# Sample states of a Mamba-2 layer turned in 32x32 blocks by VectorE instead of by TensorE

## The chip, the cores and the metric

The kernel runs on one core of a Trainium2 chip. The metric is the device time of one launch in microseconds (us). A core has four compute engines with in-order instruction queues of their own, TensorE (PE, matmuls; its weight loads are listed as PEld), VectorE (DVE), ScalarE (ACT) and GpSimd (POOL), and SyncE (SP), which here only issues DMAs. They order their work by semaphores.

## What is computed

One step of a decoder trunk for two groups that share weights: a prompt of 256 tokens, and 8 samples with 4 new tokens each (32 rows). All is float32. The layer is an HGRN2 recurrence and a Mamba-2 recurrence side by side, and then a mixture of 32 experts with the best 4 for each token. The part that matters here is the Mamba-2 recurrence of the samples, each of which brings a state `h0` of 32 heads x 64 x 128:

```
def step(h, inp):                      # one chunk; for a sample the 4 new tokens are one chunk
    xc, dtc, bc, cc = inp
    acum = jnp.cumsum(dtc * a, axis=1)
    ...
    y_inter = jnp.einsum('btgn,bgrpn->btgrp', cc, h) * jnp.exp(acum)[..., None]
    alast = acum[:, -1]
    wdec = jnp.exp(alast[:, None] - acum) * dtc
    h_new = jnp.exp(alast)[..., None, None] * h + jnp.einsum('bsgr,bsgn,bsgrp->bgrpn', wdec, bc, xc)
    return h_new, y_intra + y_inter
```

So each sample's state is read out by C (`y_inter`, a sum over the last axis n of the state), and then decayed and updated (`h_new`).

## The kernel before

The work is staged: the input projections of x, B and C with their convolution (to about 127 us of the span), the Mamba-2 preparation (127 to 160), the loop over the 8 sample states (160 to 256), the loop over 16 pairs of heads of the prompt (256 to 340), HGRN2, the output projections, router and then the experts (from about 621), whose weights stream from HBM through a ring of 9 slots of 2 MB (`wGU`, `wD`).

A state lies in SBUF as `hst[b % 4]`, 128 partitions (two heads x 64) by 16 blocks of 128 state columns n. The sum over n needs n on partitions. So for state b of the loop (`for b in range(NB)` on each engine):

- PE transposes 16 blocks of 128x128 into two PSUM banks in turn (L1905), four at a time, with a projection of the z gate (`project`, L1829, 8 matmuls of 288 columns) between the two halves. It then makes the update of the state (L1915, 16 matmuls in row tiles of 32, into banks 2 to 5), a second projection, and the read-out (L1922): one matmul of 512 columns for each group q of 4 heads' blocks, into the 32 partitions of bank 6 that belong to q. Its weights are `cmk[:, b, q, :]`, C with zeros but for sample b's four columns, so that bank 6 sums up all samples over the loop.
- ACT copies each group of four transposed blocks to `hT` (L1070), copies out the projections (`evacuate`, L1010), and now and then does an exponential or logarithm of HGRN2 (L1084 to L1096).
- POOL multiplies the state in place by its decay (L934) once it is transposed (`r_tr`).
- DVE adds the update out of PSUM to the decayed state (L1360), once POOL is done (`r_dc`) and PE is (`r_up`), then `r_ud`. Before it stands `mask` (L1350, B with the other samples' rows zeroed for the state after). After it come pieces of HGRN2's preparation, written at fixed numbers b: L1364 to L1372 at b = 1, L1374 at 2, the scans L1379 and the copies L1382 and L1383 at 4, L1385 to L1387 at 5, L1390 to L1393 at 6.
- SP stores a finished state and loads state b + 3.

`Steps` helpers such as `dstep` make an engine wait for its own instruction before. After the loop DVE weighs bank 6 by `eA` into `xdt` (L1397), and goes on to the first pair of heads (`bound`, `masked`), for whose matmuls (L1946) PE has two more projections to do first.

Of the kernel before, what the change touches and what calls it, by code (L numbers as in the profile page):

```python
# [89 lines left out]
def build(nc, x_prompt, x_sample, state_hgrn, state_ssm, state_conv, hg_lower_bounds, w_in, hg_norm_w, hg_proj,  # L90
# [24 lines left out]
    with ctx:  # L115
# [335 lines left out]
        cmk = at("cmk", 88, [P, NB, SG, 32])  # L451
# [15 lines left out]
        eA = at("eA", 187.625, [P, HPG])  # L467
# [72 lines left out]
        q_cmk = S("masked_C_ready")  # L540
        q_neg = S("scores_masked_then_identity_ready")
        r_bm = S("masked_B_ready")
        r_tr = S("state_transposed")
        r_tc = S("state_copied")
        r_in = S("state_read_out")
        r_up = S("state_update_ready")
# [201 lines left out]
        with nc.Block() as block:  # L748
# [164 lines left out]
            def _(pool):  # L913
                g = nc.gpsimd
                pstep.on(pool)
                pstep(g.memset(cmk[:], 0.0))
                for b in range(NB):
                    last = g.tensor_copy(cmk[:, b, :, NS * b:NS * b + NS], convBC[:, SG:2 * SG, SEQ + NS * b:SEQ + NS * b + NS])
                last.then_inc(q_cmk, 1)
                pool.wait_ge(q_cmk, 1)  # L920
# [10 lines left out]
                for b in range(NB):  # L931

                    pool.wait_ge(r_tr, 4 * b + 4)
# [65 lines left out]
            def _(act):  # L999
# [30 lines left out]
                evacuate(0)  # L1030
                evacuate(1)
# [4 lines left out]
                for q in range(SG):  # L1036
                    a.activation(eA[32 * q:32 * q + 32, :], av[0:32, 2, HPG * q:HPG * q + HPG], ACT.Exp)
# [24 lines left out]
                for b in range(NB):  # L1062
                    for q in range(4):
                        act.wait_ge(r_tr, 4 * b + q + 1)
                        if b > 0 and q == 0:

                            act.wait_ge(r_in, b)
                        if b == 0 and q == 0:
                            act.wait_ge(q_A, 1)
                        a.copy(hT[:, 4 * q:4 * q + 4, :], ps[:, q % 2, :]).then_inc(r_tc, 1)  # L1070
                        if q == 1:
                            evacuate(I_Z + 2 * b)
# [15 lines left out]
                    if b == 6:  # L1088
                        act.wait_ge(h_ek, 1)
                        a.activation(eT[:], eT[:], ACT.Exp).then_inc(h_x, 1)  # L1090
                    if b == 7:
# [211 lines left out]
            def _(dve):  # L1303
# [25 lines left out]
                v.tensor_scalar(nav[:], av[:], -1.0, None, ALU.mult)  # L1329
                for j in range(12):  # L1330
# [20 lines left out]

                dve.wait_ge(q_xa, 3)
                mask(0)
                for b in range(NB):
# [5 lines left out]
                    v.tensor_tensor(h, h, ps[:, 2:6, :], ALU.add).then_inc(r_ud, 1)  # L1360
                    if b == 1:
# [9 lines left out]
                        dstep(last)  # L1371
# [437 lines left out]
            def _(pe):  # L1809
# [86 lines left out]
                for b in range(NB):  # L1896
                    pe.wait_ge(q_h[b % 4], 32 * (b // 4) + 16)
                    for q in range(4):
# [8 lines left out]
                        if q == 1:  # L1907
                            project(I_Z + 2 * b)
# [482 lines left out]
```

## Time and profile before

| | |
|---|---|
| median of 3 runs | 1547.6 us (1546.91 to 1549.56) |
| span of the profiled execution | 1543.3 us |
| PE, DVE, ACT, POOL busy | 96%, 32%, 18%, 7% of the span |
| loop over the sample states | 160.1 to 255.7 us |
| POOL decays 8 states | 29.1 us |
| DVE adds 8 updates | 18.3 us |

The profile is of one execution. Its times are from the start of the span. A row of a timeline gives start and length in us, engine, line, operation, what is written and read, the shape and how many instructions were merged; in brackets stands the idle time ahead, and what ended it. A float32 matmul stands as two instructions. A matmul's length includes the way through the array, so the starts of successive rows tell how long PE was taken up.

### The profile page before, as it was taken

How to read it: one execution, taken by the hardware profiler on the slowest of the kernel's cores; microseconds unless marked ns; L12 is line 12 of the kernel's file. 1: busy time of each engine (PE TensorE's matmuls, PEld its weight loads, DVE VectorE, ACT ScalarE, POOL GpSimd, SP SyncE). 2: the span in 40 equal slices, each digit the busy share in tenths (PEclk: the TensorE clock that was granted, in tenths of full speed). 3: DMA queues.
4: the chain of work that ended last, by engine and by line, in shares of the span. 5: the costliest groups of instructions: out<-in, count | busy, mean ns of one | idle time of the engine just before them, and what ended most of it. 6: DMA issues, size and time to landing. Idle time of an engine off the chain costs nothing.

```text
span 1543.3 us, 21046 instructions
## 1 busy us (share of the span) xinstructions
PE 1482.6 (96%) x8238; PEld 757.0 (49%) x8239; DVE 490.4 (32%) x955; ACT 277.5 (18%) x618; POOL 110.5 (7%) x98
## 2 busy tenths in 40 slices
PE   9999999999999998999999999999999999899896
PEld 7777777655677764333333333333333333333332
DVE  3652455677350128222222122122122122122123
ACT  1222435532120004211010100101001100100102
POOL 1001222010140702000000000000000000000000
PEclk9999999999999999999999999999999999999998
DMA  6345487546339674999999999999999999999995
GB/s 208 110 163 173 149 262 235 197 137 199 120 103 315 242 298 173 427 427 428 427 428 428 429 428 428 428 428 428 428 429 429 428 428 428 430 428 428 429 428 223
DMA packets 105352, 507.67 MB, mean 329 GB/s; under 512 B 7575, under 2 KB 44031, under 8 KB 80575
## 3 DMA queue, kind: packets, MB, share of 16 engines
q1 hardware_dynamic: 100938, 499.37, 80.7%
q10 hardware_dynamic: 4360, 7.55, 1.5%
q8 instruction: 38, 0.62, 0.2%
q14 instruction: 16, 0.13, 0.0%
HBM read 491.18 MB, written 15.72 MB: 328 GB/s over the span
## 4 chain that ended last, share of the span: by engine, by line
PE 63%; DMA 25%; DVE 2%; ACT 1%; issue 1%; DVEq 0%; SPq 0%; ACTq 0%
DMA wGU<-in_w_gu 23%; PE ps L2325 11%; PE ps L2330 10%; PE ps L1829 10%; PE ps L2312 5%; PE ps L1842 4%; PE ps L2133 3%; PE ps L2147 2%; PE ps L2239 2%; PE ps L2160 2%; PE ps L2273 2%; PE ps L2247 1%; DMA ringS<-in_ssd_proj 1%; PE ps L1905 1%; ACT xs L1273 1%; PE ps L2260 1%
## 5 line engine op out<-in xcount | busy, mean ns | idle before, releaser
L2325 PE MATMUL ps<-wGU,xe 128*64 128x512 f32 x1536 | 342.2, 594 | 17.2 <-DMA wGU<-in_w_gu 16.5
L2330 PE MATMUL ps<-wD,aT 128*64 128x512 f32 x1024 | 226.8, 595 | 0.0
L2325 PEld LDWEIGHTS ps<-wGU,xe 128*64 128x64 f32 x1536 | 107.9, 137 | 232.8 <-issue 198.4
L1829 PE MATMUL ps<-xT,ring 128*128 128x288 f32 x704 | 179.6, 410 | 2.6 <-PEq L199 2.1
L1829 PEld LDWEIGHTS ps<-xT,ring 128*128 128x128 f32 x704 | 130.7, 190 | 42.4 <-issue 5.0
L2330 PEld LDWEIGHTS ps<-wD,aT 128*64 128x64 f32 x1024 | 70.7, 137 | 131.8 <-issue 127.9
L2312 PE MATMUL ps<-wGU,xe 128*64 128x512 f32 x512 | 121.3, 594 | 11.9 <-DMA wGU<-in_w_gu 11.9
L1725 DVE TENSOR_SCALAR sg<-sg 128x512 f32<-128x512 f32 x32 | 13.7, 427 | 333.9 <-ACT sg L1268 333.9
L1732 DVE COPY ysb<-ps 64x512 f32<-64x512 f32 x32 | 22.2, 694 | 304.0 <-PE ps L2334 304.0
L1268 ACT ACTIVATE sg<-ps 128x512 f32<-128x512 f32 x32 | 19.1, 597 | 469.6 <-PE ps L2317 469.6
L391 PE MATMUL ps<-xT,ring 128*128 128x288 f32 x320 | 78.1, 407 | 0.0
L2312 PEld LDWEIGHTS ps<-wGU,xe 128*64 128x64 f32 x512 | 36.4, 136 | 81.5 <-issue 78.4
L391 PEld LDWEIGHTS ps<-xT,ring 128*128 128x128 f32 x320 | 60.6, 190 | 17.1 <-issue 0.5
L2133 PE MATMUL ps<-ynT,ringS 128*128 128x288 f32 x256 | 62.5, 406 | 0.1
L2273 PE MATMUL ps<-ysb,gT 128*128 128x512 f32 x128 | 59.5, 606 | 0.0
L1842 PE MATMUL ps<-ring,xT 128*128 128x512 f32 x128 | 58.3, 600 | 0.0
L1280 ACT COPY ysb<-ps 64x512 f32<-64x512 f32 x32 | 18.5, 578 | 212.9 <-PE ps L2334 212.9
L2133 PEld LDWEIGHTS ps<-ynT,ringS 128*128 128x128 f32 x256 | 48.6, 190 | 13.9 <-DMA ringS<-in_ssd_proj 0.5
L2239 PE MATMUL ps<-hp,psel 128*64 128x512 bf16 x396 | 48.6, 378 | 0.2 <-DVE hp L1687 0.2
L1708 DVE TENSOR_TENSOR yacc<-yacc,ps 128x512 f32<-128x512 f32 x60 | 41.3, 688 | 21.9 <-PE ps L2273 21.9
L2273 PEld LDWEIGHTS ps<-ysb,gT 128*128 128x128 f32 x128 | 22.9, 189 | 35.1 <-issue 35.1
L1842 PEld LDWEIGHTS ps<-ring,xT 128*128 128x128 f32 x128 | 23.3, 190 | 25.7 <-issue 25.3
(476 smaller groups left out, 1451.0 us busy)
## 6 DMA issues: line engine op xcount, KB each, us to landing
wGU<-in_w_gu SPq DMA_DIRECT2D x128, 2048.0 KB, 36.7
wD<-in_w_down SPq DMA_DIRECT2D x64, 2048.0 KB, 36.8
ring<-in_w_in SPq DMA_DIRECT2D x21, 2048.0 KB, 8.8
out<-hst SPq DMA_DIRECT2D x8, 1024.0 KB, 5.8
ringS<-in_ssd_proj SPq DMA_DIRECT2D x4, 2048.0 KB, 10.0
wbuf<-prompt_A_rows ACTq DMA_DIRECT2D x16, 384.0 KB, 3.9
out<-Sb SPq DMA_DIRECT2D x2, 2048.0 KB
ring<-in_hg_proj SPq DMA_DIRECT2D x2, 2048.0 KB, 8.7
```

Of the source, the lines that this page charges most:

```text
L391: last = m.matmul(ps[:, 4 + mt, 0:T], ring[n][:, k, mt * P:(mt + 1) * P], xT[:, k, :], start=(k == 0), stop=(k == KD - 1))
L1708: v.tensor_tensor(y, y, p, ALU.add).then_inc(m_sa, 1)
L1829: last = m.matmul(ps[:, b, 0:T], ring[c % 2][:, k, n * P:(n + 1) * P], xT[:, k, :], start=(k == 0), stop=(k == KD - 1))
L1842: last = m.matmul(ps[:, b, :], xT[:, k, t0:t0 + rows], ring[c % 2][:, k, :], start=(k == 0), stop=(k == KD - 1))
L2133: last = m.matmul(ps[:, 7 - c % 2, 0:T], ringS[n % 2][:, k, (c % 2) * P:(c % 2) * P + P], ynT[:, k, :], start=(k == 0), stop=(k == XT_ - 1))
L2147: last = m.matmul(ps[:, 4 + c % 2, 0:T], ring[n][:, k, (c % 4) * P:(c % 4) * P + P], onT[:, k, :], start=(k == 0), stop=(k == HH - 1))
L2160: last = m.matmul(ps[:, b, :], mT[:, k, t0:t0 + rows], ring[n][:, k, :], start=(k == 0), stop=(k == KD - 1))
L2239: last = m.matmul(ps[half[h], B_X, :], psel[:, t, :], hp0[t][i][:, CW * h:CW * h + CW], start=False, stop=(t == 1 and i == 2))
L2273: return m.matmul(ps[:, bank, :], gT[:, t * P:(t + 1) * P], ysb[j % 2][:], start=True, stop=True)
L2312: last = m.matmul(ps[half[h], bank, :], xe[:, 2 + k, 1, :], wgu[n][:, k, col + CW * h:col + CW * h + CW], start=False, stop=False)
L2325: last = m.matmul(ps[half[h], bank, :], xe[:, f, hx, :], wgu[n][:, k, col + CW * h:col + CW * h + CW], start=(i == 0 and k == 0), stop=False)
L2330: last = m.matmul(ps[half[h], B_Y, :], aT[:, k, i - 4, :], wdn[n][:, k, CW * h:CW * h + CW], start=(i == 4 and k == 0), stop=False)
```

## The change

The state is turned on DVE. One instruction (`v.transpose`, in the program STREAM_TRANSPOSE) turns each 32x32 block of `hst` in its place and writes `hT`: partition 32j + s, block i, columns 32c + r then hold state column n = 32c + s of row 32j + r. It stands in `turn_state(b + 1)`, right after the addition to state b; that of state 0 stands ahead of the loop.

The read-out becomes 64 matmuls for a state: for each row band j, group q and n-block c one of 32 rows by 32 columns of weights, at tile position (32j, 32q), moving 4 blocks of 32 columns; the sum runs over c, and band j goes to bank j of PSUM (banks 0 to 3). Its weights `cT4` are C of all samples, laid out for each band by 16 copies on ACT after `evacuate(0)`. Every sample's rows of C are applied to state b; `gather_inter(b)` on DVE picks sample b's rows by multiplying with the selector `bs2[:, b]` and adds them up in `yin`. The update moves to banks 3 to 6, so the read-out now waits also for the addition (`r_ud`), and the next update for the gathering (`r_iy`). POOL's `cmk` and ACT's copies of `hT` are gone. `eA` is laid out anew by 8 activations instead of 4. HGRN2's pieces are spread otherwise: `kT` (L1372) now at b = 2, four scans at 4 and four at 5 with the copies, L1385 to L1387 at 6, L1390 to L1393 at 7 behind the last gathering, and ACT's exponential of `eT` at 7 instead of 6.

```diff
@@ PE, loop over the states
                 for b in range(NB):
...
-                        for c in range(4):
-                            last = m.transpose(ps[:, q % 2, c * P:(c + 1) * P], hst[b % 4][:, 4 * q + c, :], ident[:])
-                        last.then_inc(r_tr, 1)
-                        if q == 1:
-                            project(I_Z + 2 * b)
-
+                    project(I_Z + 2 * b)
                     pe.wait_ge(r_bm, b + 1)
                     if b > 0:
                         pe.wait_ge(r_ud, b)
+                        pe.wait_ge(r_iy, b)
...
                     project(I_Z + 2 * b + 1)
 
-                    pe.wait_ge(r_tc, 4 * b + 4)
-                    for q in range(4):
-                        last = m.matmul(ps[bands[q], 6, :], cmk[:, b, q, :], hT[:, 4 * q:4 * q + 4, :].rearrange("p c n -> p (c n)"),
-                                        start=(b == 0), stop=(b == NB - 1))
+                    pe.wait_ge(r_tr, b + 1)
+                    pe.wait_ge(r_ud, b + 1)
...
+                    for c in range(4):
+                        for q in range(4):
+                            for j in range(4):
+                                last = m.matmul(ps[bands[q], j, 0:P], cT4[bands[j], q, c, :], hT[bands[j], 4 * q:4 * q + 4, 32 * c:32 * c + 32],
+                                                start=(c == 0), stop=(c == 3), tile_position=(32 * j, 32 * q))
                     last.then_inc(r_in, 1)
@@ DVE
+                def turn_state(b):
+
+                    dve.wait_ge(q_h[b % 4], 32 * (b // 4) + 16)
+                    if b > 0:
+                        dve.wait_ge(r_in, b)
+                    v.transpose(hT[:].rearrange("p i n -> p (i n)"), hst[b % 4][:].rearrange("p i n -> p (i n)")).then_inc(r_tr, 1)
+
+                turn_state(0)
...
+                def gather_inter(b):
+
+                    dve.wait_ge(r_in, b + 1)
+                    part = ps[:, 0:4, 0:P]
+                    whole = yin[:].rearrange("p (j x) -> p j x", j=4)
+                    if b == 0:
+                        v.tensor_scalar(whole, part, bs2[:, 0:1], None, ALU.mult).then_inc(r_iy, 1)
+                    else:
+                        dve.wait_ge(r_iy, b)
+                        v.scalar_tensor_tensor(whole, part, bs2[:, b:b + 1], whole, ALU.mult, ALU.add).then_inc(r_iy, 1)
...
                     h = hst[b % 4][:].rearrange("p (q c) n -> p q (c n)", c=4)
-                    v.tensor_tensor(h, h, ps[:, 2:6, :], ALU.add).then_inc(r_ud, 1)
+                    v.tensor_tensor(h, h, ps[:, 3:7, :], ALU.add).then_inc(r_ud, 1)
+                    if b + 1 < NB:
+                        turn_state(b + 1)
+                    gather_inter(b)
...
-                dve.wait_ge(r_in, NB)
+                dve.wait_ge(r_iy, NB)
@@ POOL
-                    pool.wait_ge(r_tr, 4 * b + 4)
+                    pool.wait_ge(r_tr, b + 1)
@@ ACT
                 evacuate(0)
+                for c in range(4):
+                    for j in range(4):
+                        last = a.copy(cT4[bands[j], :, c, :], convBC[bands[c], SG:2 * SG, SEQ:T])
+                last.then_inc(q_c4, 1)
                 evacuate(1)
```

On PE, one state (b = 0) and the start of the next. Before, with `hst` the state, `ident` the identity, `bm` and `xw` the operands of the update, `xT` and `ring` those of a projection:

```order
91 L1905 MATMUL ps<-ident,hst_912 128x128 x8
92 L1829 MATMUL ps<-xT,ring_67 128x288 x8
93 L1905 MATMUL ps<-ident,hst_912 128x128 x8
94 L1915 MATMUL ps<-bm_919,xw_921 128x128 x16
95 L1829 MATMUL ps<-xT,ring_67 128x288 x8
96 L1922 MATMUL ps<-hT,cmk 32x512 x4
97 L1905 MATMUL ps<-ident,hst_913 128x128 x8
```

Now:

```order
91 L1850 MATMUL ps<-xT,ring_67 128x288 x8
92 L1924 MATMUL ps<-bm_920,xw_922 128x128 x16
93 L1850 MATMUL ps<-xT,ring_67 128x288 x8
94 L1937 MATMUL ps<-hT,cT_917 32x128 x64
95 L1850 MATMUL ps<-xT,ring_67 128x288 x8
```

The sixteen transposes of a state are gone, and four wide matmuls of the read-out have become 64 narrow ones.

On DVE, from the addition to state 1 to that to state 2. Before:

```order
75 L1360 TENSOR_TENSOR hst_913<-hst_913,ps 128x2048
76 L1364 RECIPROCAL lb_952<-lb_952 128x8
77 L1365 TENSOR_TENSOR lb_952<-lb_952 128x8
78 L1366 TENSOR_TENSOR lb_952<-lb_952 128x8
79 L1367 TENSOR_SCALAR lb_952<-lb_952 128x8
80 L1370 TENSOR_SCALAR eT<-eT,lb_952 128x288 x8
81 L1372 TENSOR_SCALAR kT<-eT 128x2304
82 L1350 TENSOR_SCALAR bm_920<-b_922,bs_62 128x128
83 L1360 TENSOR_TENSOR hst_914<-hst_914,ps 128x2048
```

Now:

```order
78 L1378 TENSOR_TENSOR hst_913<-hst_913,ps 128x2048
79 L1328 STREAM_TRANSPOSE hT<-hst_914 128x2048
80 L1362 SCALAR_TENSOR_TENSOR yin<-ps,bs_62,yin 128x512
81 L1385 RECIPROCAL lb_953<-lb_953 128x8
82 L1386 TENSOR_TENSOR lb_953<-lb_953 128x8
83 L1387 TENSOR_TENSOR lb_953<-lb_953 128x8
84 L1388 TENSOR_SCALAR lb_953<-lb_953 128x8
85 L1391 TENSOR_SCALAR eT<-eT,lb_953 128x288 x8
86 L1351 TENSOR_SCALAR bm_921<-b_923,bs_62 128x128
87 L1378 TENSOR_TENSOR hst_914<-hst_914,ps 128x2048
```

The turning of state 2 and the gathering of state 1 now stand ahead of HGRN2's pieces, and POOL's decay of state 2 waits for that turning.

## Rows read from the trace of the kernel before

**Rows 1.** The page: busy time of PE, and GB/s in 40 equal slices.

```profile
PE 1482.6 (96%) x8238; PEld 757.0 (49%) x8239; DVE 490.4 (32%) x955; ACT 277.5 (18%) x618; POOL 110.5 (7%) x98
GB/s 208 110 163 173 149 262 235 197 137 199 120 103 315 242 298 173 427 427 428 427 428 428 429 428 428 428 428 428 428 429 429 428 428 428 430 428 428 429 428 223
```

**Rows 2.** Waits of SP's queue, 540 to 700 us: us, times, longest.

```profile
SPq L818 <- PE ps L2160: 36.5, 2, 26.2
```

**Rows 3.** Timeline of PE, 171 to 184 us: start, length (columns as told above).

```profile
171.03 1.07 PE L1922 MATMUL ps<-hT,cmk 128*32 128x512 f32 x8
172.03 1.09 PE L1905 MATMUL ps<-ident,hst 128*128 128x128 f32 x8
172.95 4.05 PE L1829 MATMUL ps<-xT,ring 128*128 128x288 f32 x16
176.84 1.04 PE L1905 MATMUL ps<-ident,hst 128*128 128x128 f32 x8
177.80 1.17 PE L1915 MATMUL ps<-bm,xw 32*128 32x128 f32 x32
178.91 4.15 PE L1829 MATMUL ps<-xT,ring 128*128 128x288 f32 x16
182.98 1.07 PE L1922 MATMUL ps<-hT,cmk 128*32 128x512 f32 x8
```

**Rows 4.** Groups by form, 160 to 256 us: busy, mean ns, idle before.

```profile
L934 POOL TENSOR_TENSOR hst<-hst,dec 128x2048 f32<-128x2048 f32 x8 | 29.1, 3639 | 75.0 <-PE ps L1905 75.0
L1360 DVE TENSOR_TENSOR hst<-hst,ps 128x2048 f32<-128x2048 f32 x8 | 18.3, 2287 | 50.8 <-POOL hst L934 50.8
```

**Rows 5.** Timelines of PE: small matmuls of two other stages.

```profile
345.94 0.76 PE L1993 MATMUL ps<-qT,kT 128*32 128x32 f32 x64
...
415.77 1.96 PE L2079 MATMUL ps<-Sb,qsm 128*32 128x128 f32 x64
```

**Rows 6.** One line's instructions on DVE, with a PSUM operand: ns min/median/max.

```profile
L1708 DVE TENSOR_TENSOR yacc<-yacc,ps x60: 686/687/690, 676.6 to 1475.4; 128x512 f32<-128x512 f32 x60
```

**Rows 7.** Timelines of POOL and of DVE, 219 to 236 us.

```profile
225.78 3.64 POOL L934 TENSOR_TENSOR hst<-hst,dec 128x2048 f32<-128x2048 f32 x1 [8.31 <-PE ps L1905]
...
219.70 5.30 DVE L1379 TENSOR_TENSOR_SCAN eT<-keep,bT 128x288 f32<-128x288 f32 x8
...
225.55 0.22 DVE L1382 COPY lst<-eT 128x64 f32<-128x64 f32 x1
225.81 3.69 DVE L1383 COPY lst<-eT 128x64 f32<-128x64 f32 x1
229.53 0.29 DVE L1350 TENSOR_SCALAR bm<-b,bs 128x128 f32<-128x128 f32 x1
...
231.93 2.29 DVE L1385 TENSOR_TENSOR bT<-eT,mid 128x2048 f32<-128x2048 f32 x1
...
234.71 1.36 DVE L1387 TENSOR_SCALAR eT<-bT 128x2304 f32<-128x2304 f32 x1
```

**Rows 8.** Timelines of DVE, around 184 and around 339 us.

```profile
184.06 0.17 DVE L1365 TENSOR_TENSOR lb<-lb 128x8 f32<-128x8 f32 x1
...
187.52 1.36 DVE L1372 TENSOR_SCALAR kT<-eT 128x2304 f32<-128x2304 f32 x1
...
339.39 3.43 DVE L1442 TENSOR_TENSOR ynT<-ynT,ysk 128x288 f32<-128x288 f32 x1
```

**Rows 9.** Timelines of DVE and PE after the last read-out, 254 to 265 us.

```profile
255.85 2.78 DVE L1397 TENSOR_TENSOR xdt<-ps,eA 32x512 f32<-32x512 f32 x4 [0.20 <-PE ps L1922]
...
264.49 0.30 PE L1946 MATMUL ps<-ws,xdt 64*64 64x32 f32 x4
```

**Rows 10.** Timelines of ACT ahead of the loop.

```profile
139.90 0.40 ACT L1008 COPY eT<-ps 128x288 f32<-128x288 f32 x1 [6.15 <-PE ps L1829]
...
160.12 1.05 ACT L1055 COPY b<-ps 32x128 f32<-32x128 f32 x4
```

**Rows 11.** A stretch ahead of the experts: length, busy of PE, PEld, DVE, ACT, POOL, PEclk, DMA.

```profile
606.00:612.00 6.00, 2.61 (x24) 2.19 (x22) 5.38 (x17) 0.69 (x2) 0.00 (x0) 0.81 0.84 303
```

More of the change, by code:

```diff
@@ L915, in _ @@
                 pstep.on(pool)
[L916 to L920, printed above, removed]
                 pool.wait_ge(s_par, 32)
@@ L1036, in _ @@
                 for q in range(SG):
-                    a.activation(eA[32 * q:32 * q + 32, :], av[0:32, 2, HPG * q:HPG * q + HPG], ACT.Exp)
+                    for j in range(2):
+                        a.activation(eA[bands[q], :, :].rearrange("p (w j) i -> p j w i", j=2)[:, j],
+                                     av[0:32, 2, HPG * q:HPG * q + HPG].rearrange("p (i w) -> p w i", w=2), ACT.Exp)
                 a.activation(dtmp[:], dtmp[:], ACT.Exp).then_inc(q_exp, 1)
@@ L1062, in _ @@
                 for b in range(NB):
-                    for q in range(4):
[L1064 to L1070, printed above, removed]
-                        if q == 1:
-                            evacuate(I_Z + 2 * b)
+                    evacuate(I_Z + 2 * b)
                     if b == NB - 1:
@@ L1350, in mask, with scan @@
                     v.tensor_scalar(bm[b % 2][:], b2[:], bs2[:, b:b + 1], None, ALU.mult).then_inc(r_bm, 1)
+                def gather_inter(b):
[7 more added lines that the diff above has]
+                        v.scalar_tensor_tensor(whole, part, bs2[:, b:b + 1], whole, ALU.mult, ALU.add).then_inc(r_iy, 1)
+                def scan(tiles):
+                    for x in tiles:
+                        last = v.tensor_tensor_scan(eT[:, x, :], keep[:], bT[:, x, :], 0.0, ALU.mult, ALU.add)
+                    dstep(last)
                 dve.wait_ge(q_xa, 3)
@@ L1377, in _ @@
                         dve.wait_ge(h_ln, 1)
-                        for x in range(HH):
-                            last = v.tensor_tensor_scan(eT[:, x, :], keep[:], bT[:, x, :], 0.0, ALU.mult, ALU.add)
-                        dstep(last)
+                        scan(range(0, 4))
+                    if b == 5:
+                        scan(range(4, HH))
                         for x, at32, at4 in ((mid, CH // 2 - 1, 1), (lst, CH - 1, NS - 1)):
@@ L1912, in _ @@
                         pe.wait_ge(r_ud, b)
+                        pe.wait_ge(r_iy, b)
                     for c in range(4):
                         for q in range(4):
-                            last = m.matmul(ps[:, 2 + q, c * P:(c + 1) * P], xw2[bands[q], c * P:(c + 1) * P], bm[b % 2][bands[q], :],
+                            last = m.matmul(ps[:, 3 + q, c * P:(c + 1) * P], xw2[bands[q], c * P:(c + 1) * P], bm[b % 2][bands[q], :],
                                             start=True, stop=True, tile_position=(32 * q, 0))
@@ L1918, in _ @@
                     project(I_Z + 2 * b + 1)
[L1920 to L1923 removed]
+                    pe.wait_ge(r_tr, b + 1)
+                    pe.wait_ge(r_ud, b + 1)
+                    if b == 0:
+                        pe.wait_ge(q_c4, 1)
+                        pe.wait_ge(q_xa, 3)
+                    for c in range(4):
[3 more added lines that the diff above has]
+                                                start=(c == 0), stop=(c == 3), tile_position=(32 * j, 32 * q))
                     last.then_inc(r_in, 1)
```

36 lines of the change are left out of this document (13 added, 23 removed).

## Prediction

> **What bounds the kernel now.** The page first: PE is busy for 96% of the span, no other engine above a third, and from the slice at 617 us on the DMAs move 427 GB/s without a break [rows 1]. So there are two halves. To about 600 us PE works almost without a pause. After that the experts' weights stream at a fixed rate, and the end is the start of that stream plus its bytes. The stream's start follows PE, as SP's queue shows: its loads of expert weights wait for PE, 36.5 us in two waits around 550 us [rows 2]. What PE gains or loses before 600 us should therefore move the end by the same amount.
>
> The change touches one stage, the loop over the eight sample states. PE's timeline gives one state in full [rows 3], by the starts of successive rows: read-out 1.00 (171.03 to 172.03), half of the transposes 0.92, projection 3.89, the other half 0.96, update 1.11, projection 4.07, together 11.95 us (171.03 to 182.98). PE never pauses. The others do: POOL takes 3.64 us for a decay and idles 75.0 us, waiting for the transposes; DVE takes 2.29 us for an addition, and sat idle 50.8 us waiting for the decay [rows 4]. That slack is what the change spends.
>
> **What PE saves.** The transposes go (0.92 + 0.96). The projection ahead of the update now follows a matmul in column tiles, and I give it the 4.07 us of the one that stands behind the tiled update, not 3.89. So projection, update, projection are 4.07 + 1.11 + 4.07 = 9.25 us, and the new read-out comes on top.
>
> It has 64 matmuls, in the trace 128 instructions. Nothing in this trace runs on 16 tiles. Two bounds from the nearest rows [rows 5]: 64 instructions of 128 columns on four tiles take 1.96 us, 31 ns each. If sixteen tiles work side by side as these four do, a quarter of that, 128 x 7.7 = 0.98 us. If only four ever do, 128 x 31 = 3.9 us. The other row, 64 instructions of 32 columns in 0.76 us (12 ns each), shows that issuing alone needs no more than 128 x 12 = 1.5 us. I take 1.2 us, between 0.98 and 1.5, since that row excludes a slow issue and the four tiles show almost perfect overlap.
>
> A state then costs PE 9.25 + 1.2 = 10.45 us instead of 11.95: 1.5 us less, 12.0 us over eight, if it waits for nobody.
>
> **What now waits.** The new order closes a ring through three engines. Count from the end of read-out b. DVE turns state b + 1 (it needs `hT` free), POOL decays it, DVE adds the update, and only then may PE read out, since the banks overlap. No row shows a block transpose. It reads and writes 2048 elements once. Bounds: the rate of the one-operand row of 2304 elements in 1.36 us gives 1.2 us, that of the scans (5.30 us for 8 x 288, 2.3 ns an element) 4.7 us [rows 7]. I take 2.29 us, as the addition of the same size has [rows 4]. Hand-overs are 0.03 to 0.2 us, as the 0.20 ahead of L1397 [rows 9]. The ring: 0.1 + 2.29 + 0.1 + 3.64 + 0.03 + 2.29 + 0.15 = 8.6 us, against PE's 9.25 us ahead of its read-out. The spare time is 0.65 us, where before DVE alone idled for 6.4 us a state (50.8 / 8). The Trainium skill (Vector Engine (DVE) Microarchitecture Reference, 3.8 on the reshape front-end) says that the transposing array sustains one element per cycle per lane, which at 0.96 GHz is an estimated 2.1 us; no run here shows it yet, and the sum would be 0.2 us a state shorter in that ring.
>
> The gathering reads 512 elements out of PSUM, 0.69 us by the like addition [rows 6]. It comes behind the turning, and the next update needs it 3.1 us after the read-out, with PE in its projection until 4.07. It lies beside other work.
>
> **HGRN2's pieces are the term that decides.** They stand on DVE between the gathering and the next addition, that is, just while POOL decays. One place shows what then happens [rows 7]: a copy of 64 elements a partition took 0.22 us at 225.55, and the same at 225.81 took 3.69 us, to 229.50, with POOL's decay running from 225.78 to 229.42. It simply stood until POOL was done. A product with two SBUF operands did the same at 339.39: 3.43 us for 288 elements [rows 8]. Operations that read PSUM aren't held so: this is why I leave the gathering at 0.69 us. The pieces are all of the held kinds: two SBUF operands (L1365, the scans, L1385) or long one-operand ones at two elements a cycle (L1372, L1387). Each state's piece therefore begins when the decay ends, and its whole length E falls between decay and addition, with the mask (0.29) behind it. The wait on PE is E + 0.29 - 0.65:
> - behind state 1: from 184.06 to 187.52 [rows 8], E = 3.46, wait 3.10
> - behind 2: L1372 and its like L1374, 2 x 1.36 [rows 8], wait 2.36
> - behind 4: four scans, 5.30 / 2 = 2.65 [rows 7], wait 2.29
> - behind 5: four scans and four copies at a pitch of 0.26 (225.55 to 225.81), 3.65, wait 3.29
> - behind 6: 231.93 to 234.71 + 1.36 [rows 7], 4.14, no mask, wait 3.49
>
> The sum is 14.5 us. Before, all of this lay in DVE's idle 50.8 us.
>
> **Behind the loop.** DVE's products of the read-out start at 255.85, 0.20 us after PE let it go, so the last read-out ended at about 255.7. The first pair's matmuls start 8.8 us later, at 264.49, behind a chain that begins with those products [rows 9]. Now DVE first gathers (0.69) and does L1390 (1.36 by its like) with three small ones (some 0.2 each), which stood inside the loop. That is 2.7 us later, with nothing left to hide it, since PE has the same two projections as before. ACT's exponential moved to b = 7 runs beside that.
>
> **Ahead of the loop.** ACT sat idle 6.15 us before 139.90, and 16 copies at 1.05 / 4 = 0.26 us are 4.2 us [rows 10]: hidden. Four more activations of `eA` are another 1.0 us by the same price, and bound what ACT can come late by, if nothing else hides it. State 0's turning waits for its load, which was issued at the stage's start, and stands in DVE's queue ahead of work that waits for PE anyway. POOL only loses work. All of it: 0, at most 1 us.
>
> **Sum.** -12.0 + 14.5 + 2.7 = +5.2 us. The profiled execution has a span of 1543.3 us, 4.3 under the median of the runs; I set the difference against the median: 1547.6 + 5.2 = 1552.8 us.
>
> **Rivals.**
> - *The pieces run beside the decay* (faster). If only the strided copy and POOL's own collisions are held, and scans, products and masks run on, the addition waits only where turning, gathering, piece and mask outlast the decay: 3.37 + E against 6.17 us, less 0.65 of spare time, so where E exceeds 3.45. That costs 0.0, 0.2 and 0.4 us behind states 1, 5 and 6. -12.0 + 0.6 + 2.7 = -8.7: 1538.9 us. Against it stand the two held rows; for it, that the pieces are of other shapes. 0.20.
> - *The read-out doesn't use sixteen tiles* (slower). At four side by side it is 3.9 us, 2.7 more a state, and the ring shares it: +21.6, 1574.4 us; eight side by side would be about half, +7 to 1560. The point from which it alone eats the whole saving is 2.7 us. Against: the almost perfect overlap of four. 0.14. The Trainium skill (TensorEngine Tiling (Array Packing), Instruction Overhead) states some 60 cycles for each matmul, an estimated 128 x 25 ns = 3.2 us for a read-out, nearly this rival. The 12 ns above [rows 5] speak against that rule: by it that row would be twice as long.
> - *The turning is slow.* At the scans' 4.7 us the ring grows by 2.4: each of the seven turnings in the loop then costs, 2 x 1.75 where there was spare time and 5 x 2.4 elsewhere, +15.5: 1568.3 us. 0.08.
> - *The clock falls.* The granted clock was 0.81 on average, so partly at 1.2 GHz of 2.4, in a stretch where PE was busy for 2.61 of 6 us [rows 11]. Pauses of over 3 us stand in three places now. Each fall could cost PE 1 to 3 us where the ring doesn't cover it: +3 to +8 on top, about 1557.5 us. Against: the pauses are shorter than that stretch. 0.10.
>
> **How the numbers follow.** Forecast 0.48, the rivals 0.20, 0.14, 0.08 and 0.10. The forecast itself is good to some 3 us: 0.65 of spare time is a small difference of large numbers, and counts five times. So it ends within 0.2% (3.1 us, about what a measurement of this kernel can tell from no change) in perhaps a quarter of its cases, and slower in most others. Faster: 0.20 and 0.03 of the forecast's edge, 0.23. Same: 0.17. Slower: the rest, 0.60. The range takes in the first rival, the slow clock and most of the slow turning, 1537 to 1566; outside are four tiles and the worst of the turning. The forecast's own range is 1549 to 1557.
>
> **What would show each step.** PE's timeline: starts of read-outs 10.5 us apart around states 1 and 4, 12.8 to 14 behind the five pieces, with idle time of 2.3 to 3.5 us put down to DVE's addition. A read-out of 1.2 us from its start to the projection's. DVE: a turning of 2.3 us; the first operation of each piece stretched to some 3 us, ending with POOL's. First pair's matmuls 11.5 us behind the last read-out. I am wrong if the pieces keep their lengths while POOL works, if the read-out takes over 2 us, or if the stream of the experts doesn't start later by what the loop lost.

## The result and the profile after

The changed kernel takes 1563.6 us (median of 4 runs, 1562.4 to 1567.3) against 1547.9 for the kernel before: ratio 1.0115, 95% interval 1.0103 to 1.0127, so 15.7 us slower. The prediction was 1552.8 us, slower, with a range of 1537 to 1566. The sign and the decisive mechanism came true; the time is 10.8 us over the forecast and lies outside the 1549 to 1557 that I had given the forecast by itself. The profiled execution of the kernel after took 1567.3 us (span 1565.6), more than its three sisters; that of before had a span of 1543.3. The two traces are thus 22.3 us apart where the runs are 15.7, and I keep the two apart below.

First the loop over the states. The timeline of the kernel after, 165 to 196 us (start, length, engine, line; idle time ahead in brackets), answers to [rows 3] and [rows 4]:

```profile
165.61 1.17 PE L1924 MATMUL ps<-bm,xw 32*128 32x128 f32 x32
...
170.79 1.91 PE L1937 MATMUL ps<-hT,cT 32*32 32x128 f32 x128
172.63 4.15 PE L1850 MATMUL ps<-xT,ring 128*128 128x288 f32 x16
175.20 3.64 POOL L930 TENSOR_TENSOR hst<-hst,dec 128x2048 f32<-128x2048 f32 x1 [20.93 <-DVE hT L1328]
175.67 3.25 DVE L1351 TENSOR_SCALAR bm<-b,bs 128x128 f32<-128x128 f32 x1
176.71 1.17 PE L1924 MATMUL ps<-bm,xw 32*128 32x128 f32 x32
...
183.90 2.31 DVE L1328 STREAM_TRANSPOSE hT<-hst 128x2048 f32<-128x2048 f32 x1 [2.74 <-PE ps L1937]
186.14 0.71 DVE L1362 SCALAR_TENSOR_TENSOR yin<-ps,bs,yin 128x512 f32<-128x512 f32 x1
186.29 3.64 POOL L930 TENSOR_TENSOR hst<-hst,dec 128x2048 f32<-128x2048 f32 x1 [7.45 <-DVE hT L1328]
186.77 0.19 DVE L1385 RECIPROCAL lb<-lb 128x8 f32<-128x8 f32 x1
186.99 2.97 DVE L1386 TENSOR_TENSOR lb<-lb 128x8 f32<-128x8 f32 x1
187.80 1.17 PE L1924 MATMUL ps<-bm,xw 32*128 32x128 f32 x32
...
190.40 2.81 DVE L1391 TENSOR_SCALAR eT<-eT,lb 128x288 f32<-128x288 f32 x8
193.44 2.28 DVE L1378 TENSOR_TENSOR hst<-hst,ps 128x2048 f32<-128x2048 f32 x1
195.87 1.89 PE L1937 MATMUL ps<-hT,cT 32*32 32x128 f32 x128 [2.82 <-DVE hst L1378]
```

A state without a wait takes 11.10 us (176.71 to 187.80), not 11.95: the saving is there. The read-out holds PE for 1.84 us (170.79 to 172.63). POOL's decay holds DVE: a product of 8 elements a partition, issued 0.7 us into the decay, took 2.97 us and ended with it, where the next one of its size takes 0.17. Even the mask, alone beside a decay, took 3.25 us instead of 0.28. Not every operation is held: the reciprocal ahead of the product, also out of SBUF and into it, took its 0.19 us inside the decay. When the decay has ended, the rest of the piece runs, then the addition, and PE waits 2.82 us. The waits of PE by releaser, 160 to 285 us (us in all, times, longest):

```profile
PE ps L1937 <- DVE hst L1378: 12.7, 5, 3.1
```

Five waits, 12.7 us, behind the five pieces that were named.

Second, TensorE's clock. The stretches of the kernel after (length, then busy time of PE, PEld, DVE, ACT, POOL, then the granted clock, DMA share, GB/s), and two of its projections:

```profile
127.00:133.00 6.00, 3.94 (x10) 2.54 (x9) 0.28 (x2) 3.86 (x8) 0.39 (x2) 0.72 0.41 108
...
245.00:262.00 17.00, 12.71 (x192) 9.37 (x192) 14.47 (x9) 1.97 (x4) 6.55 (x2) 0.90 0.41 119
262.00:278.00 16.00, 13.73 (x172) 9.95 (x172) 12.55 (x22) 8.71 (x15) 0.00 (x0) 0.79 0.67 222
```

```profile
129.51 5.81 PE L1850 MATMUL ps<-xT,ring 128*128 128x288 f32 x16 [2.06 <-PEq L199]
...
249.78 5.43 PE L1850 MATMUL ps<-xT,ring 128*128 128x288 f32 x16
```

The granted clock is below 1 in all three stretches, partly at 1.2 GHz of 2.4, and a projection of 4.15 us takes 5.4 to 5.8. Before, the clock was full from 161 to 262 us. The one at 129.51 stands before any changed instruction of PE. It took 4.12 us in the trace of before, but in two experiments with that kernel (e2 and e9 below) the clock also fell there or 6 us later, so I don't put it down to the change. The next falls, from 249 us on, follow PE's longest wait, 3.12 us, which ended at 247.68. Not all that a slow clock adds is lost: PE waited 2.66 us for DVE after the slow projection at 249.78, and at full clock it would have been done 1.3 us sooner and would have waited 1.3 us longer.

Third, the tail of the loop. It answers to [rows 9]:

```profile
263.05 2.81 PE L1937 MATMUL ps<-hT,cT 32*32 32x128 f32 x128 [2.66 <-DVE hst L1378]
...
265.79 5.95 PE L1850 MATMUL ps<-xT,ring 128*128 128x288 f32 x16
265.90 0.75 DVE L1362 SCALAR_TENSOR_TENSOR yin<-ps,bs,yin 128x512 f32<-128x512 f32 x1 [3.00 <-PE ps L1937]
266.57 1.35 DVE L1411 TENSOR_SCALAR bT<-bT 128x2304 f32<-128x2304 f32 x1
...
268.48 2.77 DVE L1418 TENSOR_TENSOR xdt<-yin,eA 32x512 f32<-32x512 f32 x4
...
277.10 0.30 PE L1960 MATMUL ps<-ws,xdt 64*64 64x32 f32 x4 [0.67 <-DVE ws L1446]
```

The first pair's matmuls stand at 277.10 instead of 264.49, 12.6 us later, and 11.3 us behind the last read-out. From there the delay is handed on nearly whole: the router's last transposes start at 631.67 instead of 620.01.

```profile
620.01 0.74 PE L2247 MATMUL ps<-ident,xs 128*128 128x128 f32 x4 [0.68 <-ACT xs L1256]
```

```profile
631.67 0.74 PE L2261 MATMUL ps<-ident,xs 128*128 128x128 f32 x4 [0.68 <-ACT xs L1248]
```

(The first fence is of before, the second of after.) From these rows to the end of the span it is 923.3 us before and 933.9 after. So another 10.6 us are lost in a part of the kernel in which no line was changed. Two things stand out there: the queue that brings instructions (packets, MB, share of 16 engines), first before, then after, and PE's waits from 620 us on,

```profile
q8 instruction: 38, 0.62, 0.2%
```

```profile
q8 instruction: 83, 1.36, 0.4%
```

```profile
PE ps L2339 <- issue: 9.4, 5, 2.4
PE ps L2280 <- issue: 2.9, 1, 2.9
```

where before had one such wait of 0.7 us, at the first expert. So four are new at L2339, where the experts' loop has jumped back to its top, once in each turn of six experts, and one at L2280, behind the loop's end. (The clock also fell once behind one of these pauses, at 1017 us.) After, around 1014 us:

```profile
1013.88 0.39 PE L2348 MATMUL ps<-bd,esel 96*64 96x512 bf16 x2
1016.61 4.06 PE L2339 MATMUL ps<-wGU,xe 128*64 128x512 f32 x10 [2.34 <-issue]
```

Before, the same two lines follow each other 0.22 us apart:

```profile
1000.06 0.39 PE L2334 MATMUL ps<-bd,esel 96*64 96x512 bf16 x2
1000.28 3.60 PE L2325 MATMUL ps<-wGU,xe 128*64 128x512 f32 x16
```

### The profile page after: what moved, and what is told of

The parts are those of the page before. It is cut to its first block, busy times and chain, and to the rows that moved or that the text cites. A ratio compares the mean times of both kernels' runs of the same rounds, so it can differ in the third digit from the quotient of the medians.

```text
span 1565.6 us, 22710 instructions
## 1 busy us (share of the span) xinstructions
PE 1486.3 (95%) x9071; PEld 760.4 (49%) x9071; DVE 531.5 (34%) x971; ACT 263.1 (17%) x604; POOL 110.3 (7%) x89
## 3 DMA queue, kind: packets, MB, share of 16 engines
q8 instruction: 83, 1.36, 0.4%
## 4 chain that ended last, share of the span: by engine, by line
PE 63%; DMA 20%; DVE 4%; issue 2%; ACT 1%; DVEq 0%; SPq 0%; ACTq 0%
DMA wGU<-in_w_gu 20%; PE ps L2339 13%; PE ps L2344 10%; PE ps L1850 8%; PE ps L2326 5%; PE ps L2147 4%; PE ps L1863 4%; PE ps L2287 2%; PE ps L2161 2%; PE ps L2253 2%; PE ps L2174 2%; PE ps L2261 1%; PE ps L1937 1%; ACT xs L1265 1%; PE ps L2274 1%
## 5 line engine op out<-in xcount | busy, mean ns | idle before, releaser
L2339 PE MATMUL ps<-wGU,xe 128*64 128x512 f32 x1536 | 343.2, 597 | 22.5 <-DMA wGU<-in_w_gu 12.9
L2339 PEld LDWEIGHTS ps<-wGU,xe 128*64 128x64 f32 x1536 | 109.1, 137 | 239.5 <-issue 214.9
L1850 PE MATMUL ps<-xT,ring 128*128 128x288 f32 x704 | 185.2, 419 | 2.6 <-PEq L199 2.1
L2326 PE MATMUL ps<-wGU,xe 128*64 128x512 f32 x512 | 121.4, 594 | 10.8 <-DMA wGU<-in_w_gu 10.8
L391 PE MATMUL ps<-xT,ring 128*128 128x288 f32 x320 | 78.1, 407 | 0.0
```

The lines of the kernel that those rows point to most:

```text
L391: last = m.matmul(ps[:, 4 + mt, 0:T], ring[n][:, k, mt * P:(mt + 1) * P], xT[:, k, :], start=(k == 0), stop=(k == KD - 1))
L1850: last = m.matmul(ps[:, b, 0:T], ring[c % 2][:, k, n * P:(n + 1) * P], xT[:, k, :], start=(k == 0), stop=(k == KD - 1))
L2326: last = m.matmul(ps[half[h], bank, :], xe[:, 2 + k, 1, :], wgu[n][:, k, col + CW * h:col + CW * h + CW], start=False, stop=False)
L2339: last = m.matmul(ps[half[h], bank, :], xe[:, f, hx, :], wgu[n][:, k, col + CW * h:col + CW * h + CW], start=(i == 0 and k == 0), stop=False)
```

## Experiments

Every comparison is with runs of the kernel before on the same chip. The last two columns are of the profiled execution: instruction packets, and the time from the router's last transposes to the end of the span.

| kernel | median us | before us | ratio, 95% | packets | router to end |
|---|---|---|---|---|---|
| before | | | | 38 | 923.3 |
| after | 1563.6 | 1547.9 | 1.0103 to 1.0127 | 83 | 933.9 |
| e1 before, 128 instructions more | 1558.3 | 1546.8 | 1.0055 to 1.0088 | 77 | 934.6 |
| e2 before, 256 more | 1553.1 | 1546.8 | 1.0028 to 1.0062 | 39 | 926.0 |
| e3 after, 128 more | 1558.1 | 1546.8 | 1.0052 to 1.0086 | 45 | 922.8 |
| e4 after, decay on ACT | 1559.6 | 1546.8 | 1.0061 to 1.0095 | 83 | 934.2 |
| e7 after, decay split | 1555.5 | 1546.5 | 1.0037 to 1.0082 | 83 | 932.0 |
| e8 all three | 1544.3 | 1546.5 | 0.9975 to 0.9994 | 45 | 923.4 |
| e9 before, 128 more, in a wait | 1558.6 | 1546.9 | 1.0055 to 1.0088 | 77 | 934.8 |
| e10 after, 96 more, in a wait | 1559.2 | 1546.9 | 1.0053 to 1.0088 | 45 | 923.8 |
| e11 before, 60 more, in a wait | 1554.2 | 1547.3 | 1.0035 to 1.0071 | 41 | 925.7 |
| e12 before, 68 more, in a wait | 1557.1 | 1547.3 | 1.0040 to 1.0085 | 59 | 929.6 |

**Where the program lies.** In the built program PE's experts' loop is 1681 instructions of 64 bytes, from 8240 to 9920 before. The instruction packets are of 16 KB, which is 256 instructions (1.36 MB in 83 packets). Counted in such pieces from the program's start, the loop lies over seven (32 to 38) before. The change gives PE 1664 instructions more ahead of it, so after it lies from 9904 to 11584, over eight (38 to 45). Experiments 1 to 3 move the loop and do nothing else.

```
+ for _ in range(32):          # 64 in e2
+     m.matmul(ps[0:1, 3, 0:1], ebc[0:32, 0:1], ident[0:32, 0:1], start=True, stop=True)
  m.matmul(ps[0:1, 3, 0:64], ebc[0:64, 0:1], ident[0:64, 0:64], start=True, stop=True).then_inc(t_tb, 1)
```

> The kernel before, with 32 more one-column matmuls (128 PE instructions, 8 KB of program) ahead of the experts' part, and nothing else; they take under 1 us. Theory 'code': in the trace of the kernel after, 16 KB instruction packets go on all through the experts' loop (83 of them in all against 38), and PE pauses 2.7 to 3.7 us at each return to the loop's top, because the loop's 1679 PE instructions, which lie over 7 pieces of 256 in the kernel before, lie over 8 after the change. These 128 instructions put the loop of the kernel before over 8 pieces too: packets rise to 70 or more, PE pauses about 3 us at five returns, and the time rises by 5 to 10 us, to 1553 to 1558. Rival 'it is something else that came late with the stream': packets stay near 38, time 1547 to 1549.

> The kernel before with 64 such one-column matmuls (256 PE instructions, one whole piece of 16 KB), under 2 us of work. Both the extra work and the extra length are twice those of the run beside it, but the loop lies over 7 pieces again. Theory 'code' expects 38 to 40 packets, no pauses, 1547 to 1549.5 us. If the extra instructions themselves cost the time, it is later than the run with 32 of them.

> The kernel after with the same 32 one-column matmuls: its loop then lies over 7 pieces of 256 instructions. Theory 'code' expects the packets to fall from 83 to about 45, the pauses at the five returns to go, and 5 to 10 us less than the kernel after: 1554 to 1558.5 us, which is the kernel before plus what its loop over the states lost (10 to 12 us at the router). Rival 'something else': 1563 to 1565 us.

What I call five returns there are four jumps back and the loop's end. Measured: half a piece costs the kernel before 11.4 us, a whole one 6.3; the kernel after with half a piece is 11.3 us over before, not 15.7. Packets are 77, 39 and 45. With half a piece the pauses of after appear in the kernel before, and with it they go from the kernel after. Waits from 620 us on, e1 and then e3:

```profile
PE ps L2325 <- issue: 10.1, 5, 2.8
```

```profile
PE ps L2339 <- issue: 0.7, 1, 0.7
```

The last column of the table sorts all the kernels: with fetching all through the loop 932 to 935 us, without it 923 to 926. That the whole piece costs 6.3 us was not expected. Its 64 small matmuls took 3.34 us on the path, and in its trace the clock fell twice where that of before has it full: ahead of the loop over the states (1.5 us), and right behind the small matmuls, where the stretch from the router's last transposes to the same transposes of the next expert takes 21.7 us instead of 18.9 (2.8 us). Together that is 7.6 us, and the two traces are 7.2 apart. The second fall is also why its last column reads 926.0 and not 923.3. It stands in the trace of e1 too, so part of e1's 11.4 us may be the clock's and not the code's place; the runs with the matmuls in a wait, below, are without it.

I then put the small matmuls where PE waits anyway, in the router (`pe.wait_ge(t_mk, 2)`), into bank 4.

> The kernel before with 32 one-column matmuls (128 PE instructions) as in the first experiment, but in the router, where PE waits 2.75 us for DVE's masks; there they take 0.8 to 1.7 us and should cost nothing. The experts' loop then lies over 8 pieces of 256 instructions. The first experiment cost 11.4 us with 1.7 us of visible matmuls in it, the second 6.3 us with 3.3 us of them and no pauses. Theory 'code' expects 77 or so instruction packets, five pauses of 2.7 to 3.7 us, and 5 to 7 us more than the kernel before: 1552 to 1554. If what the first two experiments cost beside their own matmuls has to do with where these stood, it is 0 to 3 us.

> The kernel after with 24 one-column matmuls (96 instructions) in that same wait, so that its experts' loop lies over 7 pieces instead of 8. Nothing visible is added. Theory 'code' expects 45 instruction packets, no pauses at the returns, and the kernel after less 5 to 8 us: 1555 to 1558.5, so that the difference to the kernel before is what the loop over the states lost, 10 to 12 us less what the stream of the experts takes up. Rival 'other': 1562 to 1565.

Packets and pauses moved as the theory says (the table has the packets), the times not by what I wrote: 11.6 us more for the kernel before, where I had 5 to 7, and 12.3 over before for the kernel after, whose 1559.2 us is just above 1555 to 1558.5. The wait didn't hide the matmuls. The router's last transposes stand at 623.79 and 634.54, 3.8 and 2.9 us later than without them (1.8 of the 3.8 are a clock fall at 136 us). Less that, and if the other runs have it too, the code's place is worth 11.6 - 3.8 = 7.8 us in the kernel before. In the kernel after it is 15.7 - 12.3 + 2.9 = 6.3 by medians, and (1.0115 - 1.0071) x 1547 + 2.9 = 9.7 by ratios. The profiled executions say 10 to 11.

> The kernel before with 15 one-column matmuls (60 PE instructions) in the router's wait. Counted in the built program, the experts' loop then ends with its jump back at instruction 9980 of PE, 4 short of 9984, a multiple of 256: it lies over 7 pieces, if the pieces are counted from the program's start. Theory 'code at a border' expects 38 or 39 instruction packets, no pauses at the returns, and the kernel before plus at most the 1 to 3 us by which the like matmuls moved the router: 1547 to 1550 us.

> The same with 17 such matmuls, two more of 27 ns each: the jump back is instruction 9988, behind 9984, so the loop lies over 8 pieces. Theory 'code at a border' expects 77 instruction packets or so, pauses of some 3 us at five returns, and 7 to 10 us more than the run with 15: 1555 to 1559 us. If the border is elsewhere, the two runs are alike, and only the length by which it was crossed with 32 is known.

This was to find the border, and it isn't sharp. With 17 the loop fetched in its first turns and then stopped: 59 packets, and beside the 0.7 us at the start two waits instead of four.

```profile
q8 instruction: 59, 0.97, 0.3%
```

```profile
PE ps L2327 <- issue: 5.2, 3, 2.5
```

With 15 the profiled execution is nearly clean (41 packets; 1549.2 us; no pause at a jump back, one of 2.9 us behind the loop's end), but its other runs reach 1557.7 and the median of 1554.2 is over the 1547 to 1550 expected, and those with 17 go from 1550.3 to 1560.8. Five runs of one kernel over 8.5 us are not seen elsewhere here (four runs of another lie within 2.6 to 5.3, ten of e8 within 3.8). The difference between the two, 2.9 us, isn't one that these runs can tell. That each execution near the border decides anew how long it fetches fits this; I have one trace for each and call it likely, not shown.

The Trainium skill (Advanced Engine Details and Errata, ISA Cache) gives TensorE 128 KB in lines of 16 KB, 256 instructions, which is eight lines; the Trainium skill (Runtime: NRT & Kernel Launch, Instruction fetch mechanics) says that fetching is sequential and that a taken branch to an instruction outside the window waits for a fetch. The pauses at the jumps back agree with the second. With the first the runs agree only nearly: by eight lines a loop over eight pieces would just fit, and here seven settle (38 to 45 packets) and eight don't (77 to 83); why it is seven, no run shows. Both pages also say that only two lines are held. That doesn't agree, since by it a loop of seven pieces would fetch in every turn.

**Held by POOL.** The decay goes to ACT, 16 copies with a scale for each state:

```
- g.tensor_tensor(hst[b % 4][:], hst[b % 4][:], dec..., ALU.mult).then_inc(r_dc, 1)      # POOL
+ for i in tiles:                                                                        # ACT
+     last = a.activation(hst[b % 4][:, i, :], hst[b % 4][:, i, :], ACT.Copy, scale=dec[:, NB * i + b:NB * i + b + 1])
  for b in range(NB):
+     decay(b, range(0, 8))
      evacuate(I_Z + 2 * b)
+     decay(b, range(8, 16))
```

> The kernel after with the decay of the states taken from POOL and given to ACT, as 16 copies with a scale for each state (8 ahead of the evacuation of a projection, 8 behind it). POOL then does nothing in the loop. Theory 'held by POOL': masks, HGRN2's scans and products on DVE keep their lengths (0.28 us for a mask, 0.17 for the 128x8 product, where they were 3.25 and 2.97) and run beside the decay; the 2.0 to 3.1 us waits of PE behind five pieces (12.7 us in all) nearly go. ACT's 16 copies at the 0.26 us of its small copies are 4.2 us and an evacuation of 0.4 between, against POOL's 3.64, so the ring has 0.15 us too little and each state may wait some 0.2 us, and the ACT pieces (an exponential and its table, 4 us) may cost up to 2 us twice. Net -7 to -11 us: 1552.5 to 1556.5 us, and the first pair's matmuls at 266 to 270 us instead of 277.1. Rival 'the pieces are long by themselves or by something else': they stay as long as now and the time is 1563 or, with the longer ring, more.

Timeline, 187 to 195 us, the same piece as above:

```profile
187.43 2.45 ACT L1060 ACTIVATE hst<-hst,dec 128x128 f32<-128x128 f32 x8 [4.50 <-DVE hT L1334]
187.95 0.19 DVE L1391 RECIPROCAL lb<-lb 128x8 f32<-128x8 f32 x1
188.17 0.17 DVE L1392 TENSOR_TENSOR lb<-lb 128x8 f32<-128x8 f32 x1
...
188.78 2.81 DVE L1397 TENSOR_SCALAR eT<-eT,lb 128x288 f32<-128x288 f32 x8
...
192.54 2.29 DVE L1384 TENSOR_TENSOR hst<-hst,ps 128x2048 f32<-128x2048 f32 x1 [0.63 <-ACT hst L1060]
...
194.97 1.90 PE L1943 MATMUL ps<-hT,cT 32*32 32x128 f32 x128 [0.60 <-DVE hst L1384]
```

The product takes 0.17 us beside ACT's decay, 2.97 beside POOL's. All pieces keep their lengths; the waits fall from 12.7 us to 7 times 0.6, and the first pair's matmuls stand at 269.0. So it is POOL's decay that holds DVE; the pieces are not long by themselves. The time was 1559.6, 3 us over what I had expected: ACT's copy takes 0.305 us, not 0.26, so a state without a late table load takes 11.90 us, as long as before the change; ACT's table loads, late behind its share of the decay, cost PE 1.5 us twice, as feared; and the code's place costs the same as after. So I split the decay:

> The kernel after with POOL decaying 4 of a state's 16 tiles (0.9 us by 3.64 / 4) and ACT the other 12, five of them ahead of the evacuation of a projection and seven behind it (12 x 0.305 + 0.41 = 4.1 us, by the decay of 16 on ACT). The ring then has 2.31 + 4.1 + 2.29 + some 0.4 of hand-overs = 9.1 us against PE's 9.25, and DVE's pieces are held for no longer than the gathering anyway takes. PE's wait of 0.6 us a state, which it had with all 16 on ACT, goes: a state takes 11.1 to 11.3 us, also those with a piece; the two late table loads (1.5 us each) shrink to some 1. First pair's matmuls at about 263 to 266 us, time 1553 to 1556.5. If the pieces still cost what they do after the change, it is 1561 or more.

```profile
188.34 0.37 DVE L1396 TENSOR_TENSOR lb<-lb 128x8 f32<-128x8 f32 x1
...
194.63 1.89 PE L1947 MATMUL ps<-hT,cT 32*32 32x128 f32 x128 [0.22 <-DVE hst L1388]
...
265.54 0.30 PE L1970 MATMUL ps<-ws,xdt 64*64 64x32 f32 x4 [1.80 <-DVE ws L1456]
```

1555.5 us, the first pair at 265.5: as expected. The product is held for 0.2 us only, and PE waits 2.0 us in five places instead of 12.7. In this trace the clock did not fall between 161 and 270 us, nor in the one of all three below. It did in each of the five traces that have waits of 2 to 3.5 us (after, e3, e5, e6 and e10), two times or more, and in e4 only at 270 us. So the falls inside the loop go with the long waits; no run changes the clock alone.

**The read-out.** Two single profiled runs, in which only the read-out's own rows are used:

```
- cT4[...], hT[bands[j], 4 * q:4 * q + 4, ...]   ->   ps[bands[q], j, 0:P]
+ cT4[...], hT[bands[j], 4 * q:4 * q + 2, ...]   ->   ps[bands[q], j, 0:P // 2]      # e5
- for c: for q: for j:
+ for c: for j: for q:                                                               # e6
```

> The kernel after with a read-out that moves 64 columns in each of its matmuls instead of 128, so that the second half of what each state gives isn't computed. The number of instructions stays. The read-out takes 1.84 us from its start to the next projection's. Theory 'issue' (128 instructions by 13 to 14 ns, whatever they carry, as 64 instructions of 32 columns took 0.76 us before): it stays at 1.7 to 1.84 us. Theory 'columns' (the tiles are busy all the time): about half, 0.9 to 1.1 us, since half the columns pass.

> The kernel after with the two inner loops of the read-out exchanged: matmuls that follow each other now share the rows of the array and the bank, and differ in the column tile, where before they differed in rows and bank. Theory 'issue' expects the same 1.84 us. If neighbours in the same rows have to wait for each other, it becomes longer, up to the 3.9 us that four tiles side by side would give.

Timelines of e5, then of e6:

```profile
170.90 1.48 PE L1937 MATMUL ps<-hT,cT 32*32 32x64 f32 x128
172.31 4.15 PE L1850 MATMUL ps<-xT,ring 128*128 128x288 f32 x16
```

```profile
170.78 1.90 PE L1937 MATMUL ps<-hT,cT 32*32 32x128 f32 x128
172.61 4.15 PE L1850 MATMUL ps<-xT,ring 128*128 128x288 f32 x16
```

With half the columns it takes 1.41 us instead of 1.84: neither 1.8 nor 1.0. An instruction costs 11 ns here at 64 columns and 12 ns at 32 columns in [rows 5], nearly the same, so I read a floor of some 1.4 us from issuing. Full columns add 0.4 us on top; by what, no run shows. The order of tiles and banks makes no difference (1.83).

**All three.** The split decay; the piece of state 7 behind DVE's `bound(1)`, its exponentials on ACT behind the second pair's; and 24 small matmuls in the router's wait.

```
- if b == 7:                                    # in DVE's loop
-     dve.wait_ge(h_ek, 1)
-     v.tensor_scalar(bT[:], bT[:], EXPMAX, None, ALU.min).then_inc(h_eq, 1)
-     ...
  bound(1)
+ dve.wait_ge(h_ek, 1)
+ v.tensor_scalar(bT[:], bT[:], EXPMAX, None, ALU.min).then_inc(h_eq, 1)
+ ...
  for i in range(NPAIR + 5):
```

> The decay split as in the run beside it; state 7's piece of HGRN2 (2.0 us: an operation of 1.35 and three small ones) put behind the chain that PE's first pair waits for, with its exponentials on ACT behind the second pair's; and 24 one-column matmuls (96 instructions) in a wait of PE in the router, so that the experts' loop lies over 7 pieces of 256 instructions. By what was measured: from the kernel after, -7 to -10 for the pieces, -2 for state 7's, -5 for the code: 1546 to 1549.5 us, level with the kernel before or a little under it. If the 5 us of code don't add to the rest (transfers set the end, not PE), 1551 to 1554.

```profile
250.28 1.89 PE L1947 MATMUL ps<-hT,cT 32*32 32x128 f32 x128 [0.63 <-DVE hst L1389]
252.10 4.15 PE L1860 MATMUL ps<-xT,ring 128*128 128x288 f32 x16
...
261.61 0.30 PE L1970 MATMUL ps<-ws,xdt 64*64 64x32 f32 x4 [0.67 <-DVE ws L1451]
```

1544.3 us over 10 runs, against 1546.5 over 13 of before: 0.06 to 0.25% faster, the only version that beats it, and 1.7 us below the range that I had given. From the last read-out to the first pair it is now 9.5 us, 11.3 in e7: the moved piece gives back 1.8. From e7 to this one the medians fell by 11.2 us and the profiled executions by 10.0: 1.8 by the piece and 8.6 behind the router by the place of the code. Two more terms nearly cancel: e7's trace has a clock fall at 136 us (2.1 us) that this one has not, and from the first pair to the router this one, with the small matmuls and the moved piece there, takes 2.5 us longer.

## Why the prediction was right, and where it was short

By the terms of its sum, in the two traces:

| term | predicted | measured |
|---|---|---|
| PE saves in eight states | -12.0 | -6.8 (11.95 to 11.10 a state) |
| waits behind five pieces | +14.5 | +12.7 (14.0 at full clock) |
| behind the loop | +2.7 | +2.5 (11.3 against 8.8 us) |
| clock | 0 (a rival, +3 to +8) | +4.0 (2.7 where no wait covers it) |
| to the first pair's matmuls | +5.2 | +12.4 (observed 12.6) |
| behind the router | 0 | +10.6 in the traces, 6 to 10 by the runs |

- *The decisive term was right.* HGRN2's pieces wait for POOL's decay and PE for them. All five places came out, each wait within 0.9 us of its size: 2.82, 2.03, 2.11, 3.12 and 2.66 us against 3.10, 2.36, 2.29, 3.29 and 3.49. The last is short only by the clock: the projection ahead of it was 1.3 us slow, and at full clock the wait would have been some 3.95, over the forecast, since a second instruction of POOL's (its copy into `ws`, at 256.12) held L1407 for 0.7 us as well. That the small operations are held too was right but for the reciprocal. E4 shows the cause by taking it away. The rival in which they run beside the decay fell with the first held product.
- *The turning* was taken as 2.29 us and took 2.31; *the gathering*, taken as 0.69, took 0.71, not held, as I had argued from its PSUM operand (it starts 0.15 us before the decay; the products out of PSUM of L1336, which from 151.31 us on stand beside a decay, took no more than 0.69 us each). ACT's copies ahead of the loop were hidden.
- *The read-out was the mis-sized term.* I took 1.2 us between a bound by columns, 0.98, and one by issue, 1.5, "since that row excludes a slow issue". It doesn't: 128 instructions at the 12 ns of that row are 1.5 us, and the row is a floor, not a ceiling. Measured were 1.84: 0.64 x 8 = 5.1 us less saved. With the 1.5 that I had in hand the miss would have been 2.7 us. I chose below it, toward the overlap of the four tiles. More than four tiles do work side by side (14 ns an instruction against 31), but not at a quarter of the price; that all sixteen do, no run shows. The rival of eight side by side is in the prediction as +7; by its own rows it is (1.95 - 1.2) x 8 = 6.0, and its 1.95 us happens to be near the 1.84, but by it half the columns would have taken 1.0 us, and they took 1.41.
- *The clock* was a rival at 0.10, and came together with the forecast instead of in its place. 1.5 us of the 4.0 fell ahead of anything changed; 2.5 came behind the long waits (1.3 in the projection at 249.78, 0.3 and 0.9 in the two read-outs beside it). The 1.3 are covered by DVE's chain, as said, so that 2.7 were lost. I had argued that the waits were shorter than the idle stretch of [rows 11]; the clock fell all the same behind waits of 3.1 and 2.7 us.
- *That nothing more is lost after 600 us was wrong.* I let the stream of the experts shift by what the loop lost. It did start 11.7 us later, but took longer as well, since 1664 more instructions ahead of a loop move it against the 16 KB pieces in which instructions are brought. Nothing in my working looked at the length of PE's program, though the count of PE's instructions in [rows 1] was there.
- *Where it was luck.* The sign needed none: with the loop over seven pieces again the kernel after is still 11.3 us slower (e3). But the range reached to 1566 for a slow clock and a slow turning. The turning wasn't slow, and what brought the time to 1563.6 was mostly the read-out (5.1 us) and the code's place (6 to 10), of which the second stood nowhere in the prediction.
- *What stays open.* The traces sum to 22.3 us and the medians to 15.7. The profiled execution of after was 3.7 us over its median and that of before had a span 2 us under its usual ones; what else varies from run to run (clock falls, above all) no trace of the other runs shows. How the 10 us behind the router divide between PE's pauses (11.6 us in five, part of which a wait for weights would have filled: 28.4 us of those before, 23.7 after), the packets' share of the DMA engines (0.4% against 0.2%, some 3 us of the span) and clock falls behind the pauses wasn't separated.

## What to carry to other kernels

Before moving work from an engine to another, look at what will run beside what: an operation on VectorE that takes 0.2 us alone can cost whatever is left of GpSimd's beside it (of those seen in the loop only the reciprocal and those out of PSUM did not), and taking the GpSimd operation away, or making it short, gives that back at once. For many small matmuls, price the issue of each instruction first (11 to 14 ns here), and treat side-by-side tiles as what fills that time, not as what shortens it. And when a change adds instructions to an engine ahead of a long loop, count where the loop will lie and how many instruction packets the profile shows before and after.

## What the runs showed of the hardware

- A long loop on TensorE (1681 instructions) ran free when it lay over seven pieces of 16 KB and fetched in every turn when it lay over eight: 38 to 45 packets against 77 to 83, pauses of 1.8 to 2.8 us at each of the four jumps back and of 1.9 to 3.5 behind the loop, 6 to 11 us in all. Close to the border (60 and 68 instructions added) the times spread over 8.5 and 10.5 us; in the trace with 68 it stopped fetching after two of the jumps.
- 128 instructions of 32 rows and 32 columns of the array took 1.84 us at 128 moving columns (1.83 in the other order of the tiles) and 1.41 at 64.
- VectorE's block transpose of 128 x 2048 fp32 took 2.31 us, the time of a product of that size.
- Beside GpSimd's 3.64 us product VectorE's product and mask out of SBUF stood until it ended: 2.97 us for 0.17, 3.25 for 0.28. A reciprocal took its own 0.19, and products out of PSUM their own 0.68. Beside ScalarE's copies of the same data the held ones took their own time.
